# Delta-rule inverses: last doubling level on its one 64-block alone, gate products on VectorE, and a new order of blocks, forms and the first weight remainder

## The reference, cut to what matters

```python
def step(S, inp):
    r_t, w_t, k_t, v_t, kk_t, b_t = inp
    sa = jnp.einsum('bhvk,bhk->bhv', S, -kk_t)
    S = S * w_t[:, :, None, :] + sa[..., None] * b_t[:, :, None, :] + v_t[..., None] * k_t[:, :, None, :]
    return S, jnp.einsum('bhvk,bhk->bhv', S, r_t)
...
mean = y.mean(-1, keepdims=True)
var = jnp.square(y - mean).mean(-1, keepdims=True)
y = ((y - mean) * lax.rsqrt(var + GN_EPS)).reshape(B, T, C) * gn_g + gn_b
bonus = jnp.sum(rh * kh * r_k, -1, keepdims=True) * vh
y = (y + bonus.reshape(B, T, C)).astype(x.dtype)
return (y * g) @ w_o
```

## Time and profile before

| | us |
|---|---|
| median of 3 runs | 1445.17 |
| lowest and highest of the 3 | 1444.91, 1452.17 |
| the profiled execution, its own time | 1444.44 |
| its span, first to last instruction | 1442.6 |
| PE busy | 1348.2 (93%) |
| DVE busy | 888.7 (62%) |
| ACT busy | 606.8 (42%) |
| POOL busy | 82.5 (6%) |

### The profile page before, as it was taken

The page is one execution under the profiler, slowest core; times in us unless marked ns, Lnnn a source line. Parts: engine busy times, 40 slices in busy tenths (PEclk is TensorE's granted clock), DMA queues, the critical chain, the costliest instruction groups (busy, mean ns, idle before and its releaser), DMA issues.

```text
span 1442.6 us, 20852 instructions
## 1 busy us (share of the span) xinstructions
PE 1348.2 (93%) x8852; PEld 1202.9 (83%) x8852; DVE 888.7 (62%) x1347; ACT 606.8 (42%) x866; POOL 82.5 (6%) x56
## 2 busy tenths in 40 slices
PE   7999979799999998999999999999988998799998
PEld 4687878788999987766899998989887987699997
DVE  5257774467444465554744446998988665555555
ACT  1333332445344344444443434533444644544443
POOL 0021031002000021100200001000000000000000
PEclk9999999999999999999999999999999999899999
DMA  9333000065555537321655554644533353166650
GB/s 293 122 106 117 29 1 1 1 204 197 183 190 190 175 117 243 108 88 59 206 193 186 175 191 154 189 154 142 165 129 120 117 178 115 59 208 195 195 176 30
DMA packets 154526, 205.66 MB, mean 143 GB/s; under 512 B 7456, under 2 KB 128416, under 8 KB 154304
## 3 DMA queue, kind: packets, MB, share of 16 engines
q1 hardware_dynamic: 154432, 204.32, 43.2%
HBM read 203.26 MB, written 1.05 MB: 142 GB/s over the span
## 4 chain that ended last, share of the span: by engine, by line
PE 73%; DVE 21%; ACT 4%; issue 1%; DMA 0%; SPq 0%; DVEq 0%; ACTq 0%
PE PS L496 18%; PE PS L497 17%; PE PS L498 17%; DVE PH L2298 6%; DVE WW L1776 5%; PE PS L819 4%; PE PS L714 2%; PE PS L870 2%; DVE AL L1815 2%; PE PS L855 1%; PE PS L659 1%; DVE PA L2021 1%; PE PS L874 1%; ACT WW L1259 1%; DVE Sb L2095 1%
## 5 line engine op out<-in xcount | busy, mean ns | idle before, releaser
L1776 DVE TENSOR_TENSOR WW<-RG,WW 128x2048 fp32r<-128x2048 f32 x164 | 374.3, 2289 | 215.9 <-ACT WW L1259 215.8
L496 PE MATMUL PS<-AH,WW 128*128 128x256 f32 x1664 | 478.0, 287 | 14.6 <-DVE AL L1815 9.1
L497 PE MATMUL PS<-AL,WW 128*128 128x256 f32 x1664 | 473.3, 284 | 0.0
L498 PE MATMUL PS<-AH,WW 128*128 128x256 f32 x1664 | 473.1, 284 | 0.0
L1259 ACT ACTIVATE WW<-RG 128x2048 fp32r<-128x2048 f32 x164 | 311.3, 1906 | 89.5 <-PE PS L498 86.9
L496 PEld LDWEIGHTS PS<-AH,WW 128*128 128x128 f32 x1664 | 321.8, 193 | 21.5 <-issue 12.3
L497 PEld LDWEIGHTS PS<-AL,WW 128*128 128x128 f32 x1664 | 321.9, 193 | 1.6 <-issue 0.2
L498 PEld LDWEIGHTS PS<-AH,WW 128*128 128x128 f32 x1664 | 321.7, 193 | 0.0
L496 PE MATMUL PS<-WW,HH 128*128 128x512 f32 x304 | 118.8, 391 | 0.1
L497 PE MATMUL PS<-WW,HH 128*128 128x512 f32 x304 | 118.7, 390 | 0.0
L498 PE MATMUL PS<-WW,HL 128*128 128x512 f32 x304 | 118.3, 389 | 0.0
(11 more groups left out here) (302 smaller groups left out, 1631.7 us busy)
## 6 DMA issues: line engine op xcount, KB each, us to landing
RG<-in_ffn_w_in SPq DMA_DIRECT2D x44, 1024.0 KB, 5.1
RG<-in_w_ff SPq DMA_DIRECT2D x32, 1024.0 KB, 5.4
RG<-in_w_in SPq DMA_DIRECT2D x30, 1024.0 KB, 5.1
RG<-in_ffn_w_down SPq DMA_DIRECT2D x22, 1024.0 KB, 4.9
RG<-in_w_rkv SPq DMA_DIRECT2D x12, 1024.0 KB, 5.0
RG<-in_moba_w_qkv SPq DMA_DIRECT2D x12, 1024.0 KB, 5.5
RG<-in_w_o SPq DMA_DIRECT2D x4, 1024.0 KB, 7.9
RG<-in_wx_kv SPq DMA_DIRECT2D x4, 1024.0 KB, 5.1
```

Of the source, the lines that this page charges most:

```text
L496: e.matmul(o, lh, rh, start=start, stop=False)
L497: e.matmul(o, lh, rl, start=False, stop=False)
L498: return e.matmul(o, ll, rh, start=False, stop=stop)
L1776: v.tensor_tensor(WL[lo_n % NW], ring(SPLIT[lo_n]), WH[lo_n % NW].bitcast(F32), ALU.subtract).then_inc(s_lo, 1)
```

## The change

- The level l = 6 works on 64x64 quarters only. `invert_w` multiplies the upper left 64 rows and columns into PSUM partitions 64 to 127, 64 columns a problem; DVE copies 64x256 without a mask; `invert_xz` multiplies that with X's lower right block; ACT copies 64x256 into X's off-diagonal quarter. The constant mask of that level goes.
- The gate products move from POOL to DVE, as six instructions of 128x1024 in two calls of `gate_bonus`, between `formed(1, 0)`, `formed(1, 1)` and `formed(1, 2)`.
- `block_wide(1, ...)` on DVE comes behind `formed(1, 0)`. On PE `block_turn(1, ...)` goes behind all forms, the two groups of `outputs(0, 1)` are split by `form(1, 2)`, and banks change. `invert_w(1, 4, g)` for g < 2 waits for `s_xb` 5 + g in place of `s_at` 25 + g, and `invert_xz(1, 4, g)` for all of `s_xb`.
- ACT's `ahead('wo0', 0)` moves from behind half 1's level 5 to behind level 4; DVE's moves behind the `inverse_w` of level 6.

```diff
...
@@ -570,6 +570,7 @@
 
                 e.wait_ge(s_nv, 1)
                 e.wait_ge(s_na, 1)
+                e.wait_ge(s_yy, 4)
                 for kp in kps:
                     if kp >= 2:
                         e.wait_ge(s_mte, kp - 1)
@@ -843,7 +844,7 @@
                     e.wait_ge(s_ad, 4 * half + g + 1)
                     e.wait_ge(s_zb, 4 * half + g + 1)
                     if g < 2:
-                        e.wait_ge(s_at, (25 if half else 13) + g)
+                        e.wait_ge(*((s_xb, 5 + g) if half else (s_at, 13 + g)))
                     if half == 0 and g == 0:
                         e.wait_ge(s_tua, 2)
                 else:
@@ -852,7 +853,11 @@
                     e.wait_ge(s_wt, at - 1)
                 for n in range(4):
                     ns = slice(n * 128, n * 128 + 128)
-                    t = e.matmul(PS[g % 2][:, ns], AT[:, 4 * g + n, 0, :], Zi[:, g, ns], start=True, stop=True)
+                    if l < 6:
+                        t = e.matmul(PS[g % 2][:, ns], AT[:, 4 * g + n, 0, :], Zi[:, g, ns], start=True, stop=True)
+                    else:
+                        t = e.matmul(PS[g % 2][64:128, n * 64:n * 64 + 64], AT[0:64, 4 * g + n, 0, 64:128], Zi[0:64, g, n * 128:n * 128 + 64],
+                                     start=True, stop=True)
                 t.then_inc(s_iw, 1)
 
             def invert_xz(half, l, g):
@@ -860,14 +865,18 @@
                 at = 12 * half + 4 * (l - 4) + g
                 e.wait_ge(s_wt, at + 1)
                 if l == 4:
-                    e.wait_ge(s_xb, 4 * half + g + 1)
+                    e.wait_ge(s_xb, 8 if half else g + 1)
                 if g >= 2 or l > 4:
                     e.wait_ge(s_xz, at - 1)
                 elif half == 0 and g == 1:
                     e.wait_ge(s_bv, 4)
                 for n in range(4):
                     ns = slice(n * 128, n * 128 + 128)
-                    t = e.matmul(PS[bx][:, ns], Wi[:, g, ns], Xi[:, g, ns], start=True, stop=True)
+                    if l < 6:
+                        t = e.matmul(PS[bx][:, ns], Wi[:, g, ns], Xi[:, g, ns], start=True, stop=True)
+                    else:
+                        t = e.matmul(PS[bx][0:64, n * 64:n * 64 + 64], Wi[64:128, g, n * 64:n * 64 + 64],
+                                     Xi[64:128, g, n * 128 + 64:n * 128 + 128], start=True, stop=True)
                 if l < 6:
                     for n in range(4):
                         ns = slice(n * 128, n * 128 + 128)
@@ -903,8 +912,8 @@
                         t = e.matmul(PS[6][pp, m * 64:m * 64 + 64], BT[:, m, pp], SA[:, g, n * 64:n * 64 + 64], start=False, stop=True)
                 t.then_inc(s_st, 1)
 
-            def outputs(half, c):
-                for gg in range(2):
+            def outputs(half, c, parts=(0, 1)):
+                for gg in parts:
                     g, b = 2 * c + gg, 2 + gg
                     if c == 1:
                         e.wait_ge(s_sa, 4 * half + g + 1)
@@ -1007,16 +1016,18 @@
                     turned(1, [0, 1])
                 else:
                     turn_y(0)
-                outputs(half, 1)
-                if half == 0:
-                    for g in range(4):
-                        block_turn(1, g, 4 + g)
-                    e.wait_ge(s_tua, 4)
-                    e.wait_ge(s_xb, 6)
-                    form(1, 2, [0, 1, 4, 5])
-                    e.wait_ge(s_xb, 8)
-                    e.wait_ge(s_yy, 4)
-                    form(1, 3, [6, 7, 2, 3])
+                if half:
+                    outputs(1, 1)
+                    break
+                outputs(0, 1, (0,))
+                e.wait_ge(s_tua, 4)
+                form(1, 2, [4, 5, 0, 1])
+                outputs(0, 1, (1,))
+                e.wait_ge(s_yy, 3)
+                form(1, 3, [6, 7, 2])
+                e.wait_ge(s_at, 28)
+                for g in range(4):
+                    block_turn(1, g, (0, 1, 4, 5)[g])
 
             split_ready('wo0')
             token_piece('wo0', 4, 0, 0, ready=H_AT['y'])
@@ -1458,8 +1469,10 @@
 
             def inverted(half, l, g):
                 s.wait_ge(s_ix, 12 * half + 4 * (l - 4) + g + 1)
-                t = s.activation(Xi[:, g, :], PS[4 + (2 * g) % 4][:, :], ACT.Copy, bias=0.0, scale=1.0)
-                if l < 6:
+                if l == 6:
+                    t = s.activation(v3(Xi[0:64, g, :], 128)[:, :, 64:128], v3(PS[4 + (2 * g) % 4][0:64, 0:256], 64), ACT.Copy, bias=0.0, scale=1.0)
+                else:
+                    s.activation(Xi[:, g, :], PS[4 + (2 * g) % 4][:, :], ACT.Copy, bias=0.0, scale=1.0)
                     t = s.activation(Zi[:, g, :], PS[5 + (2 * g) % 4][:, :], ACT.Copy, bias=0.0, scale=1.0)
                 t.then_inc(s_xz, 1)
 
@@ -1538,7 +1551,7 @@
                         rows_out(1, 3)
                         s.wait_ge(s_rr_, 1)
                         s.activation(MEM[:, 1, :], MEM[:, 1, :], ACT.Copy, bias=0.0, scale=ST[:, 61:62]).then_inc(s_na, 1)
-                    if (half, l) == (1, 5):
+                    if (half, l) == (1, 4):
                         ahead('wo0', 0)
                     if (half, l) == (1, 6):
                         gn_sqrt(2, 1, 0)
@@ -1564,7 +1577,7 @@
                 outputs(half, 1)
                 if half == 0:
                     for g in range(4):
-                        block_turned(1, g, 4 + g)
+                        block_turned(1, g, (0, 1, 4, 5)[g])
             ahead('wo0', 1)
             gn_square(4, 1, 1)
             gn_sqrt(4, 1, 1)
@@ -2059,6 +2072,19 @@
                     t = v.scalar_tensor_tensor(out=rS[:, sl], in0=rS[:, sl], scalar=vec('r_k', 2 * j + m), in1=kS[:, sl], op0=ALU.mult, op1=ALU.mult)
                 t.then_inc(s_yp, 1)
 
+            def gate_bonus(c):
+
+                gn = ring('gn')
+                if c == 0:
+                    v.wait_ge(*landed('gn'))
+                    v.wait_ge(s_gta, 4)
+                    v.wait_ge(s_bv, 4)
+                own_dve(v.tensor_tensor(BV[:, c, :], BV[:, c, :], gn[:, 1024:2048], ALU.add))
+                own_dve.done()
+                own_dve(v.tensor_tensor(BV[:, c, :], BV[:, c, :], GT_[:, c, :], ALU.mult))
+                own_dve.done()
+                v.tensor_tensor(GT_[:, c, :], GT_[:, c, :], gn[:, 0:1024], ALU.mult).then_inc(s_gtg, 1)
+
             def block(half, o):
 
                 td, db = TD[half], DB[half]
@@ -2123,7 +2149,11 @@
             def inverse_w(half, l, g):
 
                 v.wait_ge(s_iw, 12 * half + 4 * (l - 4) + g + 1)
-                v.tensor_tensor(v3(Wi[:, g, :], 128), v3(PS[g % 2][:, :], 128), lvl(l), ALU.mult).then_inc(s_wt, 1)
+                if l < 6:
+                    t = v.tensor_tensor(v3(Wi[:, g, :], 128), v3(PS[g % 2][:, :], 128), lvl(l), ALU.mult)
+                else:
+                    t = v.tensor_copy(Wi[64:128, g, 0:256], PS[g % 2][64:128, 0:256])
+                t.then_inc(s_wt, 1)
 
             def state(half):
                 v.wait_ge(s_st, half + 1)
@@ -2159,7 +2189,7 @@
                     own_dve.done()
                     own_dve(v.tensor_tensor(Y3, Y3, va_.unsqueeze(2).broadcast_to([128, 8, 64]), ALU.mult))
                 if step == 6:
-                    v.wait_ge(s_gtg, 1)
+                    v.wait_ge(s_gtg, c + 1)
                     own_dve.done()
                     own_dve(v.tensor_tensor(Y, Y, GT_[:, c, half * 512:half * 512 + 512], ALU.mult))
                 if step == 7:
@@ -2185,20 +2215,22 @@
                     elif l == 5:
                         for step in (5, 6, 7):
                             group_norm(1, 0, 0, step)
-                        ahead('wo0', 0)
                         for step in (0, 1):
                             group_norm(2, 1, 0, step)
                     else:
+                        ahead('wo0', 0)
                         for step in (3, 5, 6, 7):
                             group_norm(2, 1, 0, step)
                 state(half)
                 if half == 0:
+                    formed(1, 0, [0, 1, 5])
                     for g in range(4):
                         block_wide(1, g)
-                    formed(1, 0, [0, 1, 5])
+                    gate_bonus(0)
                     formed(1, 1, [0, 1, 4, 5])
-                    formed(1, 2, [0, 1, 4, 5])
-                    formed(1, 3, [6, 7, 2, 3])
+                    gate_bonus(1)
+                    formed(1, 2, [4, 5, 0, 1])
+                    formed(1, 3, [6, 7, 2])
             for step in range(8):
                 group_norm(3, 0, 1, step)
             y_odd(0)
@@ -2461,20 +2493,6 @@
             g.wait_ge(s_bv, 4)
             g.wait_ge(s_rs_, 4)
             g.memset(SS, 0.0).then_inc(s_zero, 1)
-            g.wait_ge(s_ss, 1)
-            gn = ring('gn')
-            g.wait_ge(*landed('gn'))
-            g.wait_ge(s_gta, 4)
-            for tt in range(2):
-                for h in range(2):
-                    sl = slice(h * 512, h * 512 + 512)
```

(12 more changed lines are left out.)

1 line of the change is left out of this document (removed).

## The result

The changed kernel took 1427.44 us (median of 4 runs, 1425.12 to 1428.44) beside 1445.04 for the kernel before: a ratio of 0.9864, 95% interval 0.9832 to 0.9897. Two later comparisons of the same kernel gave 0.9848 (0.9823 to 0.9872) and 0.9846 (0.9824 to 0.9868). The profiled execution took 1428.44, its span 1426.2. The forecast was 1418.4, in a range of 1413 to 1426. The sign holds, the gain of the profiled execution is 10 us short of the forecast, and the median lies 1.4 above the range's upper end (the two later medians, 1426.24 and 1425.69, lie at it).

What follows compares the result with a forecast made beforehand. PE, busy 73% of the chain, was taken as the bound, with three waits for DVE over the delta rule. Gains of 14.4 + 12.2 - 0.6 = 26.0 us took 1444.44 to 1418.4, range 1413 to 1426.

Steps and rivals of the forecast that it cites:

- three waits: PE standing still over the delta rule for 7.78, 2.43 and 7.19 us, each time released by DVE.
- Half 1's level 6: From invert_w to solve in half 1: 18.8 us shrink to 6.6, a gain of 12.2.
- `block_wide` with POOL silent: DVE's eight block_wide instructions at half 0's end: 2.7 us, where they took 10.25 beside POOL's gate products.
- The new wait: End of half 0: PE waits 3.3 us ahead of turned, which needs all of DVE's formed(1, 1).
- no faster: Rival at level 6: 64-column quarter matmuls cost what 128 columns do now; 1424.1 us, chance 0.11.
- the forecast's own case: Whole kernel: 26.0 us less, 1418.4, with its own range 1416 to 1421; chance 0.50.
- its first rival: PE's clock falls in the wait ahead of turned, costing 2.5 us: 1420.9; chance 0.24.
- bare weight loads: Level 6 quarters: load and pass run in turn, so quarters save nothing; 1424.1 us, chance 0.11.
- dear gate products: Gate products run at POOL's rate on DVE, two calls each 4.7 us longer: 1427.8; chance 0.05.
- the changes of shape: Switches between full and quarter matmuls, 0.1 us each, four in half 0 and two in half 1: 0.6.
- the sum: Total gain: 14.4 in half 0 plus 12.2 in half 1 less 0.6 for tile shape changes, 26.0 us.
- the walk: Half 0's new order followed step by step to the end of invert_w(1, 4): 244.6 becomes 230.2, gain 14.4.

Runs made afterwards that it cites:

- the four single parts: Kernel before with one part each: earlier remainder, ratio 0.9931; level 6 on quarters, 0.9994; gate products on DVE, 0.9929; new order, 0.9968.
- the second profile of the change: The changed kernel run again without further edits, against the kernel before: 1426.24 us, ratio 0.9848.

## Why the prediction was right, and where it was not

**Right.** The bounds were read rightly: three waits, each released by DVE, and each edit met the one it was said to meet (the four single parts show it). Half 1's level 6 was forecast at 6.6 us, from `invert_w` to `solve`; it is 263.85 - 257.14 = 6.7. That this fits so well is luck in part: the two blocks of quarters took 4.2 without the wait where 3.8 stood and `rhs_of` 2.1 where 1.8 stood, and ACT's wait in the third group is 0.40 where 1.0 stood. `block_wide` with POOL silent: 2.77, forecast 2.7. Gate product: 1.22, forecast 1.22. The new wait, ahead of `turned`, released by `formed`: 2.47, forecast 3.3. Level 6 on quarters: 2.3 a block, far from the 3.7 of "no faster".

What came is not the forecast's own case, at 0.50 with 1416 to 1421, but that of its first rival: a new wait with a fall of the clock behind it, at 0.24 with 1420.9. That the range up to 1426 nearly held is luck as to the cause, for its upper end stood on bare weight loads and dear gate products, and neither came.

**The 10 us, for the profiled runs.** By the stretch the change gains 19.9 of the 26.0 forecast; 0.7 more are missing ahead of it and 3.2 behind it. Half 0, to the end of `invert_w(1, 4)`, gives 84.97 - 77.03 = 7.9 instead of 14.4; half 1 gives 12.0, with the changes of shape in it (forecast 12.2 less its part of the 0.6). The 6.5 of half 0 (6.1 beside the sum, which takes 0.4 off for its changes of shape) are:

- 3.2 from terms of the walk that were too short. In the second profile of the change, less its one fall in half 0, the gain is 11.2. The largest are `form(1, 0)` and `form(1, 3)`, 2.97 and 2.97 where about 2.0 stood: with three banks the fourth problem waits for `formed` of the first, which begins only about 1.1 us after the form does, because its matmuls of the first two problems run side by side. I had the first bank free in time. Then the two quarter blocks, 2.33 and 2.27 between starts where 1.9 stood: a quarter matmul takes 0.14, not 0.12, and a change of shape is in each block. The shorter wait gives 0.8 back.
- 1.6 from a fall of the clock in half 0's level 4, before anything of the change. The second profile of the change has no such stray fall in half 0; the third has one in half 0's level 6.
- 1.65 from the fall behind the new wait. This was the first rival. The prediction put the clock's fall "within the fourth microsecond of the wait that began at 207.3", which would leave a wait of 3.3 at the edge. Its own window shows it earlier: a granted clock of 0.53 from 210 to 211 puts the fall at 210.1, some 2.8 us into the wait. So the forecast wait of 3.3 was longer than one behind which the clock had already fallen, and by the prediction's own rows 0.24 was too low. It came in three profiles of three of the changed kernel, and at 1.65, not the 2.5 that I took from five microseconds: the lower level lasted 3.4.

Another 0.7 lie ahead of the stretch (159.65 and 160.36). And 3.2 are lost behind it: at `state` the changed kernel is 19.2 ahead, at the end of the span 16.4, in its time 16.0. All of PE's 7272 matmul records from there on are the same in both, but they don't shift as a whole. One place is a matmul behind the same wait. Before:

```profile
1118.61 0.36 PE L496 MATMUL PS<-AH,WW 128*128 128x256 f32 x1 [2.27 <-DVE AL L1821]
```

```profile
1119.00:1122.00 3.00, 3.00 (x27) 3.00 (x26) 2.13 (x4) 3.00 (x3) 0.00 (x0) 1.00 0.00 0
```

And after:

```profile
1099.47 0.55 PE L496 MATMUL PS<-AH,WW 128*128 128x256 f32 x1 [2.27 <-DVE AL L1834]
```

```profile
1100.00:1103.00 3.00, 3.00 (x18) 3.00 (x17) 2.14 (x3) 3.00 (x3) 0.00 (x0) 0.57 0.00 0
```

PE does 27 instructions in three microseconds in the one and 18 in the other; the lead shrinks by 1.3 here. The other place is near 1220. There the kernel before works at the lower level and the changed one does not, so that the lead first grows from 18.3 to 20.8:

```profile
1235.00:1240.00 5.00, 5.00 (x12) 3.55 (x12) 2.46 (x3) 4.54 (x4) 0.00 (x0) 0.50 0.01 3
```

```profile
1221.62 0.50 PE L496 MATMUL PS<-WW,AH 128*128 128x512 f32 x1 [2.37 <-DVE WW L1789]
```

Then the changed kernel's PE has to wait 2.37 us for a weight remainder on DVE, where the kernel before does not wait and the other two profiles of the change wait 0.77, and the clock falls behind it: the lead is 17.4 then, 0.9 less than ahead of it all. So a faster PE does not always bring the end nearer; DVE may decide. Over everything behind `state`, PE works 40.3 us at the lower level before and 38.1 after, and is idle for 57.1 and 60.7: in this pair the lead goes to idle time, not to the clock. In the other two profiles of the change it is the clock: idle 57.9 and 58.0, at the lower level 49.3 and 46.7, and the lead shrinks by 4.8 and 3.8.

**The steps that failed.** In the prediction's own terms there are three. "From `solve` of half 1 on, nothing is altered: it shifts as a whole": 3.2 us were lost there. The walk through half 0 had forms at 2.0 and quarter blocks at 1.9 that took 2.97 and 2.3: 3.2 us. And the sum held the clock up behind the new wait and took no stray fall into account: 3.3 us.

"The median of the runs is 0.7 above that execution, which is within their scatter, and I add nothing" names one thing more. The kernel before was forecast from a profile at the low end of its own scatter (43 later runs had a median of 1449). Beside those runs the change gains 22 us by the means, in both later comparisons, which is nearer to the forecast's 26 than the 19.6 of the first comparison.

**What the prediction did not see.** It counted the new order as part of the gain (7.8 + 2.4 of waits) and never asked what half 0 would be with the gate products alone. The row for that was there: with POOL silent `block_wide` takes 2.7, and DVE has 2 us to spare ahead of `formed(1, 0)`. The order puts `block_wide` out of that gap and onto the path. One rival to the move stays untested: gate products that stay on POOL but start later, when `block_wide` is done, would spare DVE its two calls.

## What to carry to other kernels

When several edits attack one wait, price each alone and each left out, because what they gain alone does not add up: here the move off POOL took the first wait by itself, and the reordering added for the same wait made a new one. Fill an engine's idle gap with the work that is cheap there before moving that work behind it. And where single runs differ by more than the part that is asked about, compare a stretch of the profile, with its falls of the clock counted, rather than the total.
